# A mixture-of-experts weight stream refilled by two issuing engines in place of one

## The reference, cut to what matters

```python
N_EXPERTS, TOP_K, D_FF_EXPERT = 32, 2, 512      # d_model 1024, 256 tokens
def expert_block(args):
    xb, e = args                                 # xb: the rows of h that chose expert e
    return (jax.nn.silu(xb @ w1[e]) * (xb @ w3[e])) @ w2[e]
out = lax.map(expert_block, (buf.reshape(n_blocks, MOE_BLOCK, d), blk_expert)).reshape(-1, d)
y = jax.ops.segment_sum(out[dest] * gate_sorted[:, None], tok_sorted, num_segments=n_tok)
```

## Time and profile before

| | |
|---|---|
| time, median of 3 (lowest to highest) | 1788.96 us (1788.59 to 1791.12) |
| the profiled execution: time, span | 1788.86 us, 1786.9 us |
| TensorE matmul busy | 1747.6 us (98%) |
| VectorE, ScalarE, GpSimd busy | 898.2, 695.5, 150.8 us |
| moved by DMA | 425.81 MB, mean 238 GB/s |
| the experts' stage | from 1273.8 us (first load issued) to the end |

### The profile page before, as it was taken

One profiled execution on the slowest core, in us unless ns is written; L12 is line 12 of the kernel. 1 busy time (PEld: TensorE's weight loads), 2 busy tenths in 40 slices (PEclk: granted clock), 3 DMA queues, 4 the chain that ended last, 5 costly groups with the idle time before them and its releaser, 6 DMA issues.

```text
span 1786.9 us, 30541 instructions
## 1 busy us (share of the span) xinstructions
PE 1747.6 (98%) x12532; PEld 1425.9 (80%) x12532; DVE 898.2 (50%) x1560; ACT 695.5 (39%) x1169; POOL 150.8 (8%) x156
## 2 busy tenths in 40 slices
PE   9999999999999999999999999999989999999997
PEld 8999988999999999998899999577764544445442
DVE  6655676676556765477587665375322111111111
ACT  6444544454445444455365454544321112121110
POOL 1000132210001000032322000001200000000000
PEclk9999999999999999999999999999989999999998
DMA  9555465455454555555655554421479999999996
GB/s 384 196 175 169 162 236 189 166 192 183 169 173 161 185 176 178 168 204 196 236 188 179 186 189 142 105 65 44 190 305 404 421 422 421 422 421 423 422 422 262
DMA packets 89177, 425.81 MB, mean 238 GB/s; under 512 B 17504, under 2 KB 34144, under 8 KB 42976
## 3 DMA queue, kind: packets, MB, share of 16 engines
q1 hardware_dynamic: 88624, 421.01, 62.8%
q10 hardware_dynamic: 432, 3.10, 0.4%
HBM read 423.03 MB, written 1.05 MB: 237 GB/s over the span
## 4 chain that ended last, share of the span: by engine, by line
PE 84%; DMA 5%; SPq 5%; ACT 2%; DVE 2%; issue 1%; POOL 0%; POOLq 0%; DVEq 0%; ACTq 0%
PE ps L657 18%; PE ps L659 18%; PE ps L658 18%; PE ps L1270 8%; SPq L591 4%; PE ps L1313 4%; DMA ring<-stream_expert 3%; PE ps L1251 2%; PE ps L982 2%; PE ps L994 2%; PE ps L1227 2%; DMA con<-stream_expert 2%; PE ps L751 1%; PE ps L988 1%; PE ps L835 1%
## 5 line engine op out<-in xcount | busy, mean ns | idle before, releaser
L1778 DVE TENSOR_TENSOR w_split<-ring,w_split 128x1024 fp32r<-128x1024 f32 x335 | 425.0, 1276 | 340.2 <-ACT w_split L1367 339.4
L657 PE MATMUL ps<-x_hi,w_split 128*128 128x272 f32 (+1 forms) x1856 | 541.2, 292 | 3.2 <-DVE x_lo L1783 1.6
L659 PE MATMUL ps<-x_hi,w_split 128*128 128x272 f32 (+1 forms) x1856 | 534.2, 288 | 0.0
L658 PE MATMUL ps<-x_lo,w_split 128*128 128x272 f32 (+1 forms) x1856 | 532.0, 287 | 0.0
L1367 ACT ACTIVATE w_split<-ring 128x1024 fp32r<-128x1024 f32 x335 | 350.6, 1054 | 359.9 <-PE ps L659 358.6
L657 PEld LDWEIGHTS ps<-x_hi,w_split 128*128 128x128 f32 x1856 | 349.6, 188 | 15.4 <-issue 8.9
L658 PEld LDWEIGHTS ps<-x_lo,w_split 128*128 128x128 f32 x1856 | 349.6, 188 | 0.4
L659 PEld LDWEIGHTS ps<-x_hi,w_split 128*128 128x128 f32 x1856 | 349.5, 188 | 0.0
L659 PE MATMUL ps<-hid_hi,w_split 128*128 128x272 f32 (+1 forms) x704 | 201.6, 286 | 0.0
L658 PE MATMUL ps<-hid_lo,w_split 128*128 128x272 f32 (+1 forms) x704 | 201.5, 286 | 0.0
L657 PE MATMUL ps<-hid_hi,w_split 128*128 128x272 f32 (+1 forms) x704 | 201.2, 286 | 0.0
(11 more groups left out here) (407 smaller groups left out, 2189.1 us busy)
## 6 DMA issues: line engine op xcount, KB each, us to landing
ring<-stream_expert SPq DMA_DIRECT2D x132, 1024.0 KB, 23.0
ring<-stream_ffn SPq DMA_DIRECT2D x131, 1024.0 KB, 4.9
arena<-stream_expert SPq DMA_DIRECT2D x40, 1024.0 KB, 24.0
ring<-stream_in SPq DMA_DIRECT2D x27, 1024.0 KB, 5.0
ring<-stream_mod SPq DMA_DIRECT2D x24, 1024.0 KB, 7.1
con<-stream_expert SPq DMA_DIRECT2D x20, 1024.0 KB, 23.5
ring<-stream_out SPq DMA_DIRECT2D x12, 1024.0 KB, 5.0
ring<-stream_in SPq DMA_DIRECT2D x42, 256.0 KB, 3.8
```

Source lines behind the costliest of these rows:

```text
L657: pe.matmul(to, w[:, 0, k], hi, start=first, stop=False)
L658: pe.matmul(to, w[:, 0, k], lo, start=False, stop=False)
L659: return pe.matmul(to, w[:, 1, k], hi, start=False, stop=last_)
L1778: nc.vector.tensor_tensor(w[:, 1], half_of(n), w[:, 0].bitcast(fp32), ALU.subtract).then_inc(split_ready, 1)
```

## The change

ScalarE takes over the refills of the even units (10, 12, ..., 94), SyncE keeps the first nine units and the refills of the odd ones (9, 11, ..., 95). SyncE's refills wait for `big_done` as before. ScalarE's have no wait of their own: each stands behind a copy of `pair(n)` or `rows(n)` that has already waited for TensorE. Behind `pair(n)` it issues both halves of unit 6n + 10 (over b = 1 of pair n) and of unit 6n + 12 (over b = 3), and behind `rows(n)` those of unit 6n + 14 (over b = 5): six DMAs a pair, 86 in all; SyncE has the other 88. The last three pairs of ScalarE's loop are written out, because their refills end with unit 94.

```diff
             def experts(pass_):
                 for unit, q in units(RING_SLOTS, 2 * RING_SLOTS):
-                    again(pass_, 0, unit, q)
+                    if unit % 2 == 1:
+                        again(pass_, 0, unit, q)
                 with sp.Fori(1, TURNS) as i:
                     for unit, q in units(0, 2 * RING_SLOTS):
-                        again(pass_, i, unit, q)
+                        if unit % 2 == 1:
+                            again(pass_, i, unit, q)
                 for unit, q in units(0, BIG_SLOTS):
-                    again(pass_, TURNS, unit, q)
+                    if unit % 2 == 1:
+                        again(pass_, TURNS, unit, q)
...
+            def refill(i, unit):
+                turn, unit = divmod(unit, TURN * BIG_SLOTS)
+                u, b = divmod(unit, BIG_SLOTS)
+                for q in range(2):
+                    part = slice(q * BIG_HALF, (q + 1) * BIG_HALF)
+                    act.dma_start(big_slot(u, b, BIG)[:, part],
+                                  stream_expert[(i + turn) * TURN + u, b, :, part]).then_inc(big_full[big_landed(u, b, q)], 16)
...
             def pairs(pass_):
                 gathered_tokens(pass_ * PAIRS)
-                with act.Fori(0, TURNS) as i:
+                with act.Fori(0, TURNS - 1) as i:
                     for u in range(TURN):
                         n = pass_ * PAIRS + i * TURN + u
                         pair(n)
+                        refill(i, u * BIG_SLOTS + 1 + RING_SLOTS)
+                        refill(i, u * BIG_SLOTS + 3 + RING_SLOTS)
                         rows(n)
+                        refill(i, u * BIG_SLOTS + 5 + RING_SLOTS)
+                for u in range(TURN):
+                    n = pass_ * PAIRS + (TURNS - 1) * TURN + u
+                    pair(n)
+                    for b in (1, 3):
+                        if u * BIG_SLOTS + b + RING_SLOTS < (TURN + 1) * BIG_SLOTS:
+                            refill(TURNS - 1, u * BIG_SLOTS + b + RING_SLOTS)
+                    rows(n)
+                    if u * BIG_SLOTS + 5 + RING_SLOTS < (TURN + 1) * BIG_SLOTS:
+                        refill(TURNS - 1, u * BIG_SLOTS + 5 + RING_SLOTS)
                 pair(pass_ * PAIRS + PAIRS - 1, False)
```

## The result

Eight runs of each kernel on the same chip gave medians of 1794.94 us after (1794.19 to 1796.61) and 1788.78 us before (1787.32 to 1791.12). The ratio is 1.0035, 95% interval 1.0025 to 1.0045: slower by 6.2 us. The prediction was 1795.9 us, +6.9.

The account below looks back on a forecast made before the run. The load stream at 422 GB/s was taken to bound the kernel, by its end and the last needed half's place. Terms 4.4 + 2.5 + 0 + 0 = +6.9 us on 1788.86 gave 1795.8, as median 1795.9 us; range 1788.5 to 1803.5.

Parts of the forecast that it names:

- What bounds the stage: Experts' stage: the load stream at 422 GB/s sets the time, slower than TensorE by 2.4 us a pair.
- Term 1: First pair's refills: ScalarE requests units 10, 12 and 14 later, so the stream ends 4.4 us later.
- Term 2: End of the stream: fewer halves follow the last needed one with two queues; +2.5 us, bounds 0 to 5.0.
- the lone half: End of the stream: about one half of ScalarE's runs alone, after one shared pair; 2.5 us.
- Units of one parity: Loads in the profile after: if units of one parity are always the late ones, Term 2 is wrong.
- a queue that drifts: End of the stream: ScalarE's queue falls three units behind; +14.5 us, 1803.5 us; over +10 has chance 0.22.
- Term 3: ScalarE's refill issues: their time is hidden behind its waits for TensorE; 0 us.
- Term 4: Whole stream: a second queue leaves the rate at 422 GB/s; 0 us.
- the rate rival: Whole stream: two queues lift the rate; at 438 GB/s -9 us, 1780 us; chance 0.12.
- some 7: TensorE's last up half in the profile after: it comes some 7 us later.

Follow-up runs that it names:

- e9_prompt_half: e1_prompt with unit 90's second half refilled by SyncE instead of ScalarE; 1796.44 us, +7.6 us against the kernel before.
- e2_onequeue: The kernel before, all loads on SyncE, but even units' refills wait for the ScalarE events that release them in the changed kernel; 1794.42 us, +5.4.
- e3_rows: The changed kernel with all six of ScalarE's refills a pair put behind `rows(n)`; 1802.19 us, +13.1 us against the kernel before.
- e1_prompt: The changed kernel with ScalarE's refills of units 10 and 12 moved up, behind the Silu and the hidden rows' copy; 1789.23 us against 1789.07 before.
- e11_tail: The changed kernel with the last pair's six units all refilled by SyncE in the order of use; 1792.78 us, +3.9 against the kernel before.
- e4_last: The changed kernel with unit 94, the last even one, refilled by SyncE; 1795.32 us, +6.3 us against the kernel before.
- e8_half: The changed kernel with unit 90's second half refilled by SyncE instead of ScalarE; 1794.98 us, +6.1 us against the kernel before.

## Why the prediction was right

**What bounds the stage.** Right. The stream stands at 422 GB/s in both kernels, and the time of the kernels follows the gaps at its start and the place of the last needed half. Where a kernel departs from that, as e9_prompt_half does by its clock, it is said.

**Term 1, the late requests, +4.4.** 4.0 measured, by the sixty-us window and by the end of the stream. No further gap came: 422 GB/s over the whole flat stretch. e2_onequeue has the term without the second queue, e3_rows twice of it, e1_prompt none of it. Issue times came at 1348.75 and 1355.78, where 1347.4 and 1354.7 were forecast; less the 1.7 us by which the stage began later, within 0.7.

**Term 2, the order at the end, +2.5.** 2.5 measured, and e11_tail takes it back. The end came as forecast: three halves follow unit 92's second half (94's two and 95's second), with unit 94's last half alone at the very end. But the lone half didn't come from where I had it, so the size is in part luck. I had counted it from the first burst, with ScalarE alone in the stream for 1.2 halves before it and 84 halves against 84.8 left. In the trace two of ScalarE's halves landed ahead of SyncE's next, and units 12 to 15 land level. The step arose at ScalarE's second burst, where I had asked only whether the stream would have a gap, and not whether ScalarE's queue would run empty by itself. And what keeps unit 92's second half late is what stands ahead of it in its own queue, not what stands behind; e4_last, e8_half and e9_prompt_half each missed what I expected of them until this was seen. Units of one parity were the late ones: ScalarE's even ones in after, SyncE's in e8_half. The prediction named a queue that drifts as its weakest place. In e3_rows and e9_prompt_half the lead did reach three halves.

**Term 3, ScalarE's time, 0.** Right, by L1748's wait of 4.90 us, unchanged, and issues of 0.33 to 0.48 us with none blocked. One thing that I said it would show was wrong: the wait was to fall from 4.9 to about 3. The four issues do lie inside it, but an issue isn't counted as busy, so the number can't fall.

**Term 4, the rate, 0.** Right. The queues of after from 1360 to 1770 us (packets, MB, share of the 16 engines):

```profile
DMA packets 23745, 172.91 MB, mean 422 GB/s; under 512 B 2642, under 2 KB 2642, under 8 KB 2642
q1 hardware_dynamic: 11938, 86.92, 51.0%
q10 hardware_dynamic: 11801, 85.91, 50.2%
```

Half each and 422 GB/s together, as forecast; the rate rival is out. The Trainium skill (DMA: Bandwidth & Descriptors, rules for kernel authors) says that spreading transfers over issuing engines gives no bandwidth; this trace agrees with its 422 against 422.

**What the trace shows besides.** TensorE waits for loads longer (the waits of after in the gate and up products for loads into `ring`, in us, times and the longest):

```profile
PEld ps L1273 <- DMA ring<-stream_expert: 11.2, 6, 2.5
PE ps L1273 <- DMA ring<-stream_expert: 8.8, 10, 1.6
```

They were 4.5 and 5.9 us before; with the loads into `con` and `arena` the second line is 12.2 us after and 7.8 before. The first wait for a load ends at 1578.92, stage time 251, and before at 1655.19, stage time 329. That is 78 us, 2.8 pairs of 27.4 us, and two were forecast. The last up half came 6.5 us later in stage time, "some 7" was forecast. Of it 0.5 was given back behind (13.5 to 13.0): the stand at the branch, with no loads left to move, is 1.0 us shorter, and the down product 0.5 longer.

## What to carry to other kernels

When a stream of loads runs at its full rate, an edit to who issues it is worth only two things: the moments in which no request is waiting, and how many pieces land after the last one that is waited for. Write down the time at which each request can go out, and put no request behind an instruction of another engine's schedule that ends later than its buffer comes free; here a refill stood 13.7 us behind its free buffer and cost 4 us once, and asking one queue in the order of freeing at the start, and in the order of use at the end, won 2.2. Two queues that share a stream don't keep the order of use between them. A queue that runs empty lets the other get ahead even when the stream has no gap, so ask that question of each queue by itself. Give the last pieces to one queue, or check in the trace which queue leads before moving anything.

## What the runs showed of the hardware

**Two queues of equal loads land in step.** Loads of 1 MiB on SyncE's and ScalarE's queues landed in pairs every five us (1763.1 from SyncE and 1763.3 from ScalarE; 1773.1 and 1772.8), each in twice the 2.5 us that it takes alone. The packets are taken in equal turn, as the earlier trace rows had it on 34 to 36 us: 11938 against 11801 of them from 1360 to 1770. A lead arises when one queue runs empty: in after SyncE's queue got ahead near 1376, when ScalarE's had run empty. The lead then stayed one half from unit 16 to the end of the stream, 390 us, and in e3_rows three halves; nothing evened it out.

**SyncE's issues stopped blocking.** SyncE's rows of after in the experts' stage:

```profile
L591 SPq DMA_DIRECT2D ring<-stream_expert x72: 327/333/682, 1275.8 to 1741.6; - x72
```

The longest is 0.68 us, where it was 6.3 with the median at 0.43. Issue and landing times tell when it blocks. Before, 88 of its loads were issued while ten or more of its earlier ones hadn't landed, and 75 of these issues took over 1 us; of the 104 with nine or fewer outstanding none took over 0.69. After, SyncE never had more than 7 outstanding and ScalarE never more than 8. It was worth nothing here, since a request that gets earlier into a full stream only waits there.

**A wait can cost more than its length.** In e9_prompt_half TensorE stood for 6.27 us, in which its granted clock fell from 1.00 to 0.50, and then took 6.03 us for 16 products that take 3.7: 2.3 us on top of the wait. In the flat stretch of after, where no product waited longer than 1.6 us, the granted clock stayed at 1.00.
